# Scores of two heads in one PSUM bank, with the mask added by TensorE, in the first attention's second kind of heads

## What is computed

```python
qb = qr[:, i * 64:(i + 1) * 64]                 # queries, scaled by HEAD_DIM ** -0.5
ss = where(valid_s, einsum('bqghd,bgqkld->bghqkl', qb, kg), -inf)
ps = softmax(ss)                                # selected branch ("slc")
o_s = einsum('bghqkl,bgqkld->bqghd', ps, vg)
sw = where(valid_w, einsum('bqghd,bsgd->bghqs', qb, kwb), -inf)
pw = softmax(sw)                                # window branch ("win")
o_w = einsum('bghqs,bsgd->bqghd', pw, vwb)
return gate[0] * o_c + gate[1] * o_s + gate[2] * o_w
```

## Time and profile before

| | us |
|---|---|
| median of 3 runs | 1352.73 |
| lowest and highest | 1351.6, 1353.11 |
| the profiled execution, its own time | 1355.96 |
| its span | 1354.3 |
| mean granted TensorE clock over the span | 0.993 of 2.4 GHz |

### The profile page before, as it was taken

How to read it: one execution, slowest core, us unless ns; L and a number is a source line. 1 busy time by engine, 2 the same in 40 slices (tenths; PEclk the granted TensorE clock), 3 DMA queues, 4 the chain that set the end, 5 groups by cost and what they waited for, 6 DMA issues and landing times.

```text
span 1354.3 us, 18984 instructions
## 1 busy us (share of the span) xinstructions
PE 1330.4 (98%) x7306; PEld 823.3 (61%) x7306; DVE 641.7 (47%) x1224; ACT 243.1 (18%) x573; POOL 89.1 (7%) x114
## 2 busy tenths in 40 slices
PE   9999999999999999999999999999999999999996
PEld 8677575786747856586686675744444444444433
DVE  1226589877862257977979263421221222212213
ACT  2135311211102450120123162100000000000002
POOL 1116500000000120000000100000000000000001
PEclk9997999999999999999999999999999999999999
DMA  9931154565453414676574405399999999999994
GB/s 381 354 109 65 64 205 178 219 237 216 183 197 150 157 45 190 236 292 263 221 276 168 158 34 216 147 421 419 421 421 413 422 421 421 422 420 421 421 421 195
DMA packets 51006, 359.53 MB, mean 265 GB/s; under 512 B 5888, under 2 KB 6096, under 8 KB 8432
## 3 DMA queue, kind: packets, MB, share of 16 engines
q1 hardware_dynamic: 45248, 324.60, 59.5%
q0 software_dynamic: 5392, 32.05, 6.6%
q10 hardware_dynamic: 288, 1.80, 0.3%
HBM read 356.88 MB, written 1.05 MB: 264 GB/s over the span
## 4 chain that ended last, share of the span: by engine, by line
PE 82%; DVE 7%; issue 1%; ACT 1%; DVEq 0%; ACTq 0%
PE ps L1470 13%; PE ps L980 13%; PE ps L971 11%; PE ps L1499 7%; PE ps L1395 7%; PE ps L1448 7%; PE ps L953 5%; PE ps L794 4%; PE ps L799 2%; PE ps L873 2%; PE ps L892 1%; PE ps L831 1%; PE ps L1355 1%; PE ps L1224 1%; PE ps L1241 1%
## 5 line engine op out<-in xcount | busy, mean ns | idle before, releaser
L2698 DVE TENSOR_TENSOR masked_and_probs<-ps,gate_rows 128x512 f32<-128x512 f32 x52 | 33.5, 686 | 152.4 <-PE ps L1499 152.4
L794 PE MATMUL ps<-xT,ring 128*128 128x256 f32 x432 | 94.7, 380 | 0.8 <-DVE xT L1992 0.8
L1448 PE MATMUL ps<-masked_and_probs,probT 128*128 128x512 f32 x208 | 94.4, 594 | 1.0 <-DVE masked_and_probs L2698 1.0
L1395 PE MATMUL ps<-masked_and_probs,mix_rows 128*128 128x256 f32 (+1 forms) x416 | 93.0, 376 | 0.0
L1395 PEld LDWEIGHTS ps<-masked_and_probs,mix_rows 128*128 128x128 f32 x416 | 75.0, 190 | 28.8 <-issue 19.6
L971 PEld LDWEIGHTS ps<-xT,ring 128*128 128x128 f32 x768 | 87.8, 192 | 3.8 <-issue 3.8
L1607 ACT ACTIVATE qk_tiles<-ps 64x256 f32<-64x256 f32 (+3 forms) x84 | 39.2, 468 | 278.0 <-PE ps L971 241.8
L794 PEld LDWEIGHTS ps<-xT,ring 128*128 128x128 f32 x432 | 81.5, 190 | 12.3 <-ACT xT L1595 1.0
L971 PE MATMUL ps<-xT,ring 128*128 128x128 f32 x768 | 88.7, 275 | 0.0
L980 PE MATMUL ps<-ring,qk_tiles 128*128 128x512 f32 x192 | 85.2, 592 | 0.0
L953 PE MATMUL ps<-ring,xT 128*128 128x512 f32 x192 | 83.8, 593 | 0.0
(11 more groups left out here) (469 smaller groups left out, 2260.8 us busy)
## 6 DMA issues: line engine op xcount, KB each, us to landing
ring<-in_stream SPq DMA_DIRECT2D x200, 1024.0 KB, 8.6
qk_tiles<-in_stream SPq DMA_DIRECT2D x46, 1024.0 KB, 20.3
v_rows<-in_ada POOLq DMA_DIRECT2D x12, 1024.0 KB, 5.1
qk_tiles<-in_ada POOLq DMA_DIRECT2D x12, 1024.0 KB, 5.2
vec_rows<-in_stream SPq DMA_DIRECT2D x12, 1024.0 KB, 17.2
con<-in_stream SPq DMA_DIRECT2D x12, 1024.0 KB, 18.2
y_rows<-in_stream SPq DMA_DIRECT2D x12, 1024.0 KB, 19.7
par<-in_stream SPq DMA_DIRECT2D x12, 1024.0 KB, 20.8
```

What stands on the lines that cost most here:

```text
L794: mm = pe.matmul(ps[0:n, bank, off:off + T], w[:, kk, col:col + n], src[:, k, :], start=bank not in started, stop=k == KT - 1, skip_group_ ...
L1395: mm = pe.matmul(ps[:, 5 + kk // 2, kk % 2 * 2 * P:kk % 2 * 2 * P + width], h2[:, t, k * P:(k + 1) * P], select[:, t, 0:width], start=t == ...
L1448: mm = pe.matmul(ps[:, q, :], probT[:, buf, 256 + q // 2 * P:256 + (q // 2 + 1) * P], yslot[:, q % 2 * 512:(q % 2 + 1) * 512], start=False ...
L2698: dve.tensor_tensor(yslot[:, cols], ps[:, 5 + half, :], gaterow[:, 1, cols], ALU.mult).then_inc(ready, 1)
```

## The change

In units 16 to 47 the heads of a branch are taken in the order 0, 2, 1, 3, 4, 6, 5, 7. A pair (0 and 2, 1 and 3, ...) has its scores side by side in one PSUM bank. TensorE adds the mask to them there, by a product of the identity with `hidden` (128 by 128, +1e30 where a key is hidden), which ScalarE makes once at the start; the scale of -1/8 is now in the keys, by the copies that take them out of PSUM. VectorE takes both minima in one reduction of the PSUM bank, and writes no masked scores; ScalarE's exponentials read the scores from PSUM. The transposes of a pair share a bank and follow together, at i - 4, VectorE copies both heads at once, and the sums of both follow at i - 6. The scores of a pair wait for the exponentials that read their bank before. Units 0 to 15 and the other stages stay as they are.

```diff
--- before.py
+++ after.py
@@ attention_units: the two kinds "slc" and "win" @@
-            for h in range(8):
+            for h in (0, 2, 1, 3, 4, 6, 5, 7):
@@ constants @@
-TWO_BANKS = 34
+TWO_BANKS = 36
+PAIRED = range(16, 48)
@@ shared helpers @@
+def sum_column(u):
+    kind, _, h, _, _, _, g = UNITS[u]
+    first = group_units(g)[0]
+    return first + h - UNITS[first][2] if kind in ("slc", "win") else u
+        hidden = causal[:, 0, P:2 * P]
+        def pair_scores(u):
+            p, nk = u // 2, UNITS[u][3]
+            bank = p % 2 if u < TWO_BANKS else (0, 1, 6, 7)[p % 4]
+            return ps[:, bank, 0:2 * nk].rearrange("p (n k) -> p n k", n=2)
+        def pair_turned(u):
+            return ps[:, 2 + u // 2 % 2, 0:2 * UNITS[u][3]]
...
@@ TensorE @@
+            def wait_scores_read(u):
+                if u < INSTANCES["a0"][1]:
+                    if u == PAIRED[0]:
+                        pe.wait_ge(s_mask, u)
+                    elif u > PAIRED[0] + 2:
+                        pe.wait_ge(s_exp, u - 2 if u < TWO_BANKS else u - 6)
...
+            def masked_scores(u, pair):
+                def mask(n):
+                    qt, nk = UNITS[u + n][1], UNITS[u + n][3]
+                    return pe.matmul(scores(u + n)[:, qt * P:nk], ident, hidden, start=False, stop=True, skip_group_check=True)
+                for n, (lhs, keys) in enumerate(pair):
+                    pe.matmul(scores(u + n), lhs, keys[0][0], start=True, stop=False, skip_group_check=True)
+                    mm = mask(n)
+                mm.then_inc(s_sc, 2)
+            def turn_pair(u):
+                pe.wait_ge(s_exp, u + 2)
+                if u == PAIRED[0] and u < INSTANCES["a1"][0]:
+                    pe.wait_ge(s_pTsb, u - 1)
+                elif u >= PAIRED[0] + 2:
+                    pe.wait_ge(s_pTsb, u - 2)
+                for n in range(2):
+                    for t in range(UNITS[u][3] // P):
+                        mm = pe.transpose(turned_bank(u + n)[:, t * P:(t + 1) * P], prob[:, (u + n) % 4, t * P:(t + 1) * P], ident)
+                mm.then_inc(s_pT, 2)
...
-                for i in range(a, b + (4 if name == "a0" else 5)):
+                for i in range(a, b + 5):
...
-                        if i >= 2:
+                        if i in PAIRED:
+                            wait_scores_read(i)
+                        elif i >= 2:
...
+                        if i in PAIRED:
+                            masked_scores(i, pair)
...
+                    u = i - 4
+                    if a <= u < b and u in PAIRED and u % 2 == 0:
...
+                        turn_pair(u)
...
+                    u = i - 6
+                    if name == "a0" and a <= u < b and u in PAIRED and u % 2 == 0:
+                        row_sums(u)
+                        row_sums(u + 1)
...
-                        pe.wait_ge(s_mask, b - 2)
+                        pe.wait_ge(s_exp, b - 4)
                         turn_rows(mix, "mix0", 0)
@@ ScalarE @@
-                        act.activation(prob[:, u % 4, 0:nk], masked[:, u % 4, 0:nk], ACT.Exp, bias=negmax[:, u:u + 1],
-                                       scale=-1.0, accum_out=esum[:, u:u + 1]).then_inc(s_exp, 1)
+                        act.activation(prob[:, u % 4, 0:nk], scores(u) if u in PAIRED else masked[:, u % 4, 0:nk], ACT.Exp, bias=negmax[:, u:u + 1],
+                                       scale=-1.0, accum_out=esum[:, sum_column(u):sum_column(u) + 1]).then_inc(s_exp, 1)
...
+            copy(hidden, causal[:, 0, 0:P], scale=-1.0)
...
-            copy(kvraw[:, 0, :], ps[:, 1, 0:T])
+            copy(kvraw[:, 0, :], ps[:, 1, 0:T], scale=-SCALE)
...
-                copy(kvraw[:, 1, :], ps[:, 6, 0:T])
+                copy(kvraw[:, 1, :], ps[:, 6, 0:T], scale=-SCALE)
@@ VectorE @@
-                for i in range(a, b + (6 if name == "a0" else 7)):
-                    if i < b:
+                for i in range(a, b + 7):
+                    if i < b and i in PAIRED and i % 2 == 0:
+                        dve.wait_ge(s_sc, i + 2)
+                        dve.tensor_reduce(negmax[:, i:i + 2], pair_scores(i), AX, ALU.min).then_inc(s_mask, 2)
+                    if i < b and i not in PAIRED:
...
+                    u = i - 4
+                    if a <= u < b and u in PAIRED and u % 2 == 0:
+                        dve.wait_ge(s_pT, u + 2)
+                        dve.tensor_copy(pair_probs(u), pair_turned(u)).then_inc(s_pTsb, 2)
...
-                    u = i - (5 if name == "a0" else 6)
+                    u = i - 6
```

More of the change, by code:

```diff
@@ L236 @@
 ROPE_AT = (12, 16)
+PAIRED = range(16, 48)
 def by_scalar(u):
-    return u % 4 == 1 and (UNITS[u][0] == "loc" or UNITS[u][0] == "fox" and UNITS[u][1] == 1)
+    return u % 4 == 1 and u not in PAIRED and (UNITS[u][0] == "loc" or UNITS[u][0] == "fox" and UNITS[u][1] == 1)
 def taken_before(u, scalar):
     return sum(by_scalar(w) == scalar for w in range(u + 1))
+def sum_column(u):
+    kind, _, h, _, _, _, g = UNITS[u]
+    first = group_units(g)[0]
+    return first + h - UNITS[first][2] if kind in ("slc", "win") else u
 def group_units(g):
@@ L597, in factors, with pair_probs @@
             return mix[:, 1, 0:512]
+        def pair_probs(u):
+            if u < INSTANCES["a1"][0]:
+                buf = probT[:, u // 2 % 2, :]
+            else:
+                buf = (probT[:, 0, :], probT[:, 1, :], mix[:, 0, 0:512], mix[:, 0, 512:1024])[u // 2 % 4]
+            return buf[:, 0:2 * UNITS[u][3]]
         def turned_probs(u):
+            if u in PAIRED:
+                return pair_probs(u)[:, u % 2 * UNITS[u][3]:(u % 2 + 1) * UNITS[u][3]]
             if u < INSTANCES["a1"][0]:
@@ L605, in scores @@
         def scores(u):
+            if u in PAIRED:
+                return pair_scores(u)[:, u % 2, :]
             return ps[:, u % 2 if u < TWO_BANKS else (0, 1, 6, 7)[u % 4], :]
@@ L843, in turn_factors, with row_sums @@
                 mm.then_inc(s_fT, 1)
+            def wait_scores_read(u):
[4 more added lines that the diff above has]
+                        pe.wait_ge(s_exp, u - 2 if u < TWO_BANKS else u - 6)
+                elif u >= INSTANCES["a1"][0] + 8:
+                    pe.wait_ge(s_exp, u - 6)
+            def masked_scores(u, pair):
[16 more added lines that the diff above has]
+                mm.then_inc(s_pT, 2)
+            def row_sums(u):
+                _, _, _, vals = unit_operands(u)
+                _, _, _, nk, col, w, g = UNITS[u]
+                wait_probs(u)
+                if u == group_units(g)[0] and g >= 2:
+                    pe.wait_ge(s_odone, g - 1)
+                for t, val in enumerate(vals):
+                    n = min(P, nk - t * P)
+                    mm = pe.matmul(ps[:, 4 + g % 2, col:col + w], turned_probs(u)[0:n, t * P:(t + 1) * P], val,
+                                   start=t == 0, stop=t == len(vals) - 1)
+                if u == group_units(g)[-1]:
+                    mm.then_inc(s_o, 1)
             def attention(name, pieces=None):
                 a, b = INSTANCES[name]
-                for i in range(a, b + (4 if name == "a0" else 5)):
+                for i in range(a, b + 5):
                     if i < b and i % 2 == 0:
@@ L864, in attention @@
                             pe.wait_ge(s_projsb, 12)
-                        if i >= 2:
+                        if i in PAIRED:
+                            wait_scores_read(i)
+                        elif i >= 2:
                             pe.wait_ge(s_mask, i if i < TWO_BANKS + 2 else i - 2)
                         pair = [unit_operands(i + n)[:2] for n in range(2)]
-                        for k in range(len(pair[0][1])):
+                        if i in PAIRED:
+                            masked_scores(i, pair)
+                        for k in range(len(pair[0][1]) if i not in PAIRED else 0):
                             for n, (lhs, keys) in enumerate(pair):
@@ L875, in attention @@
                                     mm.then_inc(s_sc, 1)
-                    if i == b + 4:
+                    if i == b + 4 and name != "a0":
                         turn_factors(UNITS[b - 1][6])
@@ L879, in attention @@
                         turned_sums(i - 6)
+                    u = i - 4
+                    if a <= u < b and u in PAIRED and u % 2 == 0:
+                        if u == INSTANCES["a1"][0]:
+                            pe.wait_ge(s_foxk, 2)
+                        turn_pair(u)
                     u = i - 3
-                    if u == a and name == "a1":
+                    if u == a and name == "a1" and u not in PAIRED:
                         pe.wait_ge(s_foxk, 2)
-                    if a <= u < b:
+                    if a <= u < b and u not in PAIRED:
                         nk = UNITS[u][3]
@@ L897, in attention @@
                     u = i - 4
[L898 to L910, removed]
+                    if name == "a0" and a <= u < b and u not in PAIRED:
+                        row_sums(u)
```

(10 more changed lines are left out.)

4 lines of the change are left out of this document (added).

## The result

| | before | after |
|---|---|---|
| median of 6 runs beside each other | 1352.92 | 1398.12 |
| lowest, highest | 1351.6, 1354.46 | 1367.52, 1399.36 |
| mean granted clock, lowest and highest time | | 0.998, 0.973 |
| the profiled execution, its own time | 1355.96 | 1399.22 |
| its span | 1354.3 | 1397.5 |

The changed kernel is slower: 1.0151 times the time before, 95% interval 1.0099 to 1.0204. That ratio leaves out the runs of the kernel that are over 1.5% above its fastest; here these are four of six, they came again in two later sets, and the rest of this text explains them and so counts them. I had forecast 1363.7 with a range up to 1369.5. The direction was right; the measured time lies above the range.

A forecast was written before the change was run, and what follows sets the result against it. TensorE, busy 98% of the span, was taken to bound the kernel. Second half +5.8 and first half -1.1 gave +4.7 at full clock; +6.3 for low clock made +11.0: profiled 1355.96 to 1367.0, median 1363.7, range 1355 to 1369.5.

The forecast's parts named there:

- (d): Attention-stage scores waiting for exponentials of the pair before the last: costs nothing, up to 0.5 us in a narrow pair.
- (b): VectorE, per wide pair: one minimum and one copy of 512 columns, 0.68 us each, some 0.3 us less.
- (c): ScalarE's exponentials reading PSUM instead of SBUF: unchanged at 0.51 us, 0.6 per head with the sums' read.
- (a): Scores and masks on TensorE: wide pair 0.63 to 1.73 us, narrow 0.42 to 1.32, +16.0 us over sixteen pairs.
- third rival: Each added change of rows also waits for TensorE's pipe to empty, 0.17 us each, +5.4: 1369.1; chance 0.11.
- the clock falls again for the same 13.7 us: Attention stage after the thirty-column products: half clock for 13.7 us again, losing 6.3 us.
- Rival 1: The clock stays at full through the attention stage: +4.7 us, 1357.4; chance 0.19.

The follow-up runs named there:

- a_third: The changed kernel itself, unaltered, run again on a chip with two other variants; six runs from 1366.21 to 1400.41 us, ratio 1.0163, profiled run 1366.61.
- e4: The changed kernel without the mask products in these units, so the mask is left out; 1368.24 us (1360.69 to 1376.52, four runs).
- e3: The changed kernel with both heads' score products first, then both masks, second score product without start flag; 1361.21 us, ratio 1.0048.
- e8: The changed kernel with score products over all 128 rows, each score summing two heads; 1385.35 us, with more mixture-of-experts work; stage 41.7 us.
- a_again: The changed kernel itself, unaltered, run once more; 1378.74, 1401.06, 1397.51 and 1366.94 us, profiled run 1378.74.
- e7: The kernel before with the sixteen thirty-column products split into two halves of eight; 1352.79 us, ratio 0.9999.
- e6: The changed kernel with the sixteen thirty-column products split into two halves of eight; 1366.0 us, ratio 1.0101.
- e5: The kernel before with only the order of heads changed, and the columns of the sums to suit; 1363.08 us, ratio 1.0077.
- e10: The changed kernel with four more dense 512-column products ahead of the two compressed sums; 1369.96 us once, 1381.34 to 1383.0 five times, ratio 1.019.
- e2: The kernel before with two added dense 512-column products behind the compressed scores; 1356.16 us, ratio 1.0001.

## Why the prediction was wrong

**What bounds the stage: right.** TensorE did before, and does after; the added waits cost nothing ((d) held: in the stage TensorE's matmuls waited for ScalarE only ahead of the first scores, 0.4 us as before, and for VectorE once, 0.3 us, in the profiled execution and in a_third, at full clock, alike). (b) held with 0.69 and 0.69 for 0.68, (c) with 0.47 for 0.51.

**Step (a), the price of a change of rows: wrong, 5.4 us.** I read 0.63 us for a wide pair before as two loads of 0.105 and two streams, and concluded that nothing was left for a wait behind them. The sum was right and the split wrong: only one load stands in it (the two heads' loads go to different rows), and the rest is the wait until the array is empty before the transposes load. Both readings give 0.63 for that row, and part where there are four changes in a group. The runs decide: at full clock e4's narrow scores of two heads, on one half of the rows, take 0.63, which is four streams of 0.112, one load, and 0.08 left for the emptying. By a_third: 1.57 = 0.90 of columns + 4 loads (0.42) + three waits of some 0.085. By e3: 1.18 = 0.90 + 2 loads + one wait of 0.07. By e8, no change: 0.89. The fourth wait of a pair lies between sums and the next scores (119.63 to 120.12: 0.49 for four instructions of 0.098), and my sum of the pair had left it out too. 64 waits (four in each of 16 pairs) x 0.085 = 5.4, and 47.9 + 5.4 = 53.3, which is what a_third shows. That is my third rival's mechanism, with half its price for each and twice its number; that its +5.4 is the same is luck. The rule of the Trainium skill that I had set aside there (TensorEngine Tiling (Array Packing), Key Properties: a change of tiling mode drains TensorE) holds in e3 and e8; the row at 143.37 couldn't have told it from what I took it for.

**Step "the clock falls again for the same 13.7 us": wrong, and the larger part of the loss.** Where it fell, it did so within some 2 us of the end of the thin products (before 116.6; after 117.1, a_again 119.0), but then it stayed low for 27.3 or 71.7 us, and in a_third it didn't fall. The 27.3 cost 12 us of time (1379 less 1367), the 71.7 cost 32 (1399 less 1367), in line with 1.85. I had taken the end of the low stretch from the row where it ended before, the dense products at 129.13, as if they would always end it. In the changed kernel they come after twice as much low time and are sometimes not enough; what stands between them and the end of the stage is score and mask groups. In the profiles the clock rose in stretches without 64-row scores or within 1 us behind them; the changed stage has few long ones, and such a stretch alone is not enough (140.67 to 146.78, after). So the step failed on the length; what decides the length stays open. Of the 32.2 us between the forecast for the profiled execution (1367.0) and its time (1399.2), about 26 are this step's (32 or so lost to the clock, where I had 6.3) and 5.4 those of (a).

**The low clock's price before: wrong by 2 us.** I reckoned that 13.7 us at half clock lose 6.3. The profiled execution took 1355.96, those at 0.998 take 1351.5: it loses 4.4. There TensorE waits for VectorE in part, and those waits are shorter when TensorE is slower: ahead of the wide scores and their sums e7 has 1.44 us of them at full clock (listed above), the kernel before at half clock 0.43 (0.16 ahead of 116.99 and 0.27 ahead of 122.62). The base at full clock is thus 1351.5, and the stage, as an estimate, since no profile has the kernel before at full clock throughout, 43.2 - 4.4 = 38.8. (e7 gives 39.0: its stage of 43.65 with 10.2 us low, less 4.7 by the ratio.) So the change costs 14.5 us at full clock (53.3 - 38.8; e6, 1366.0 less 1351.5, says the same), where the forecast's own numbers give 47.9 - (43.2 - 6.3) = 11.0.

**The base: wrong by about 3 us.** I took the profiled execution's 3.2 us above the median off the forecast, as if they had nothing to do with the clock; they are part of the 4.4 that its low clock cost. Rival 1 shows it: +4.7 at full clock counts from the profiled execution, so its time was 1360.7 and not 1357.4, and with the 5.4 of step (a) that is 1366.1, as measured.

**Chances.** "Slower" got 0.81 and holds. The range failed since it took the length of the low clock (10 to 20 us) from one execution; the rivals had it at 0 or 13.7, and none at more. Rival 1 by name (full clock, 1357.4) came in 4 of 16 runs, at 1366 to 1368. Those four times lie inside my range by luck: the 5.4 that I had left out stand there in place of the 6.3 of a low clock that didn't come.

## What to carry to other kernels

Price a change between fp32 products of 64 and of 128 rows at about 0.19 us of TensorE at full clock (a load of 128 columns, 0.105, and the emptying; e8 gives 11.6 / 64 = 0.18), each way, and put products of the same rows behind each other: e3 got back 6 us by order alone. When work is moved onto a TensorE that already bounds, count its columns, and count too what is lost if the new order keeps two heads from running side by side (e5: 2.4 us for eight pairs). Where the granted clock has a low stretch anywhere in the profile, treat its length as unknown rather than as measured, and time many runs: the change's own time may have several levels.

## What the runs showed of the hardware that I hadn't expected

- TensorE without a gap stayed at 1.2 GHz for 71.7 us (after), 51.2 us (e4) and 27.3 us (a_again). The Trainium skill, TensorE: Matmul & The Clock Gate, section "What's actually happening", lets sustained activity release the throttle; here being busy, as the profile counts it, was not enough by itself. The clock rose in or within 1 us behind dense 512-column products (before 130.3, e5 137.0, e7 131.6, a_again 146.3, e10 145.2), in transposes and sums (e2 126.8), or some us after the last 64-row scores (after 188.8, e4 167.4). Which property of the work decides is open: e8, all 128 rows, was at full clock in the whole stage in its profile, and e4, with fewer 128-row products than the changed kernel, was low in every run.
- The length of the low stretch differs between executions of one program on one chip, in three levels for the changed kernel (none, 27.3 or 71.7 us), with 30 us of time between the ends. The kernel before has no such levels: 13.7 us in its one profile, and mean clocks from 0.992 to 0.998 with several between.
- A change between 64 and 128 rows costs a wait of 0.07 to 0.09 us as well as the load of 0.105; see e3 and e8.
